# Attention weights turned as pairs of half tiles of 64 rows into one pair of PSUM banks, four score banks, and another order of scores, turns and copies after the gate tiles

## The chip, the cores and the metric

The kernel runs on one core of a Trainium2 chip. The metric is the device time of one execution in microseconds (us). All arithmetic is in fp32. The core's engines run their own programs side by side: TensorE (PE in the profile), VectorE (DVE), ScalarE (ACT), GpSimd (POOL) and SyncE (SP), and they wait for one another by semaphores.

## The reference, cut to what matters

One block of gated linear attention and delta-rule layers is followed by two layers of attention over 512 tokens. The change is in the attention part of those two layers only. For each block of 128 queries and each head it computes (q, k and v differ by kind of attention):

```
logits = einsum('bnqghd,bnkgd->bnghqk', qb, kb) * dh ** -0.5
logits = where(mask, logits + bias, NEG)
p      = softmax(logits, axis=-1)          # times a gate for two kinds
out    = einsum('bnghqk,bnkgd->bnqghd', p, vb)
mixed  = concat([o_a, o_b, o_c], -1) * silu(z)
```

## The kernel before

The two attention layers run one behind the other (l = 0, 1). In each, the attention is cut into 40 jobs (JOBS, NJ = 40), ten (PER) for each block qb of 128 queries. A job holds two heads, e = 0 and 1. Its kind says how many keys it has: "slc", "win" and "mla" jobs have nb = qb + 1 blocks of 128 keys, "swa" jobs two blocks (one for qb = 0). In a query block the kinds stand in this order: slc, win, swa, slc, win, swa, mla, swa, mla, swa. A job with nb of at most 2 is "narrow", else it is wide.

A job j passes through the engines like this:

- TensorE `score(j)`: one matmul for each head into a PSUM bank of its own. For slc, win and swa the contraction has 64 rows, and the two heads use different rows of the array; for mla it has 96 rows.
- VectorE `least(j)` (L2928): adds the bias, writes the negated logits to PB in SBUF, and takes the row minimum, once for each head.
- ScalarE `expo(j)` (L3050): the exponential in place and the row sum, once for each head.
- VectorE `norm(j)` (L2934): the reciprocal of the two sums.
- GpSimd `normed(j)` (L3107, L3109): multiplies the weights by it.
- TensorE `turn(j)` (L2822): transposes the weights, one 128 x 128 block at a time, into PSUM. A narrow job has one bank for both heads, a wide one a bank for each head.
- VectorE or ScalarE `out_of_psum` (L2915, L3060): copies the turned weights to PT in SBUF. Of a wide job VectorE copies head 0 and ScalarE head 1; a narrow job is copied whole, by VectorE when j is even and by ScalarE when j is odd.
- TensorE `product(j)`: the weights times the values, nb x 2 matmuls into banks 6 and 7.

All engines step through one loop i = 0 .. 45. In step i TensorE scores job i, turns job i - 4 (TURN) and forms the product of job i - 6 (PV); the other engines copy job i - 4 in the same step, and VectorE takes the reciprocal of job i - 1. Even and odd steps have opposite orders. In steps 0 to 11 TensorE also fills the gate tiles (four 128 x 512 matmuls a step, banks 2 and 5); FILLED = 12. Up to step 12 the score banks are 0 and 1 and the turn banks 3 and 4 (`few`); from step 13 on they are (2, 0, 1) and (5, 3, 4) (`all_`), each taken in turn. `ps.take` makes TensorE wait until the tile that was last in the bank has been copied out; `ps.take_two` does so for two neighbouring banks and gives them to one tile. PB holds 5 jobs (NJP) and PT holds 3 (NJT), so `least(j)` waits until job j - 5 has been turned.

GpSimd also forms sums of the output weights (L2045) between jobs in steps 14 to 37, and once a scaling (L3128). VectorE also does `gated` (L2964), `least_cmp`, `norm_cmp` and `out_cmp` (L2942 to L2956) for a small compressed attention, once per query block. After step 45 TensorE goes on with the output projection, some 46 us of dense matmuls.

Of the kernel before, what the change touches and what calls it, by code (L numbers as in the profile page):

```python
# [112 lines left out]
def program(nc, I, out):  # L113
# [2622 lines left out]
    TURN, PV = 4, 6  # L2736
    CMP_EXP, CMP_SUM, CMP_TURN, CMP_PV = 1, 2, 5, {1: 0, 4: 1}
# [42 lines left out]

    def ends(j):

        return {8: 0, 9: 1}.get(j % PER)

    def attn_t(t, l):
        meet(t, f"qkv{l}")
        few = itertools.cycle((0, 1)), itertools.cycle((3, 4))
        all_ = itertools.cycle((2, 0, 1)), itertools.cycle((5, 3, 4))
# [18 lines left out]
        def score_cmp(qb):  # L2807
            p = ps.take(t, "scc", l, qb, bank=next(rings[0]))
            for a in range(2):
                x = mm(t.go, p[:, 64 * a:64 * a + 64], qT[:, a, 128 * qb:128 * qb + 128], KC, True, True)  # L2810
            x.then_inc(st, nt("scc", l, qb))

# [20 lines left out]
        def product(j):  # L2833
# [8 lines left out]
            for b in range(nb):  # L2842
                for e in range(2):
                    if kind == "mla":
                        vv = VM[:, k0 + b, 2 * a + e, :]
                    else:
                        v0 = {"slc": 0, "win": 64, "swa": 140}[kind]
                        vv = VN_[:, k0 + b, v0:v0 + 64]
                    x = mm(t.go, o[64 * e:64 * e + 64, c], vv, PT[j % NJT][:, e, 128 * b:128 * b + 128],
                           b == 0 and kind != "win", b == nb - 1)  # L2850
# [7 lines left out]
        def turned(i):  # L2858
            qb, at = divmod(i, PER)
            if TURN <= i < NJ + TURN:  # L2860
                turn(i - TURN)
            if qb < 4 and at == CMP_TURN:
                turn_cmp(qb)
# [19 lines left out]
        for i in range(NJ + PV):  # L2883
            rings = few if i <= FILLED else all_
            if i % 2 == 0:
                turned(i), filled(i), scored(i), summed(i)
            else:
                summed(i), scored(i), filled(i), turned(i)
# [14 lines left out]
    def out_of_psum(e_, sem, count, write, l, j, e):  # L2903
# [3 lines left out]
        e_.wait_ge(st, nt["pT", l, j, e])  # L2907
# [3 lines left out]
        if e == "both":  # L2911
# [4 lines left out]
        ps.empty(sem, count, "pT", l, j, e)  # L2916

    def attn_v(v, l):
        meet(v, f"qkv{l}")

        def least(j):
            qb, kind, a = JOBS[j]
            k0, nb, nk, at = keys_of(qb, kind)
            for e in range(2):
                v.wait_ge(st, nt["s", l, j, e])
                if j >= NJP:
                    v.wait_ge(st, nt["pT", l, j - NJP, "both" if narrow(j - NJP) else e])
# [46 lines left out]
        for i in range(NJ + PV):  # L2974
            for m in gates_in(i - 1)[1] if i else ():
                out_gate_v(v, l, m)
            if i % 2 == 0:
                turned(i)
# [3 lines left out]
            if i % 2:  # L2982
                turned(i)
# [55 lines left out]
    def attn_a(a_, l):  # L3039
# [23 lines left out]
        for i in range(NJ + PV):  # L3063
            if i % 2 == 0:
# [3 lines left out]
            if i % 2:  # L3068
# [193 lines left out]
```

## Time and profile before

| | |
|---|---|
| median of 3 runs | 1321.39 us (1321.22 to 1321.66) |
| the profiled execution, its own time | 1320.69 us |
| its span, first to last instruction | 1318.9 us |
| TensorE busy | 1273.5 us (97% of the span) |
| VectorE, ScalarE, GpSimd busy | 694.4, 413.4, 395.4 us |
| mean granted TensorE clock | 0.995 |
| steps 13 to 45 of the first layer | about 878 to 956 us of the span |
| the same steps of the second layer | about 1183 to 1261 us |

The profile is read by engine: who is busy in a stretch, and who waited for whom. A busy TensorE is not one at its peak, since overlapping matmuls count as busy until they have drained. "Granted clock" 1.00 is TensorE's upper level of 2.4 GHz, 0.50 its lower one of 1.2 GHz.

### The profile page before, as it was taken

What the parts mean: (1) busy time and instruction counts of PE and PEld (TensorE: products, weight loads), DVE (VectorE), ACT (ScalarE), POOL (GpSimd) and SP (SyncE); (2) the same over time, 40 slices, a digit from 0 to 9 for tenths busy, and PEclk for the clock granted to TensorE, in tenths of its full rate; (3) what the DMA queues carried; (4) which work ended last, traced back from release to release, by engine and by line L of the source; (5) the groups of instructions that cost most, each with busy time, mean ns of one, the idle gap of its engine ahead of it and who ended that gap; (6) DMA issues with size and microseconds to landing.
All of it is one profiled execution on the core that took longest, in us unless ns stands there. A gap on an engine that the chain in (4) does not pass through costs nothing.

```text
span 1318.9 us, 24624 instructions
## 1 busy us (share of the span) xinstructions
PE 1273.5 (97%) x9971; PEld 778.4 (59%) x9971; DVE 694.4 (53%) x1422; ACT 413.4 (31%) x898; POOL 395.4 (30%) x470
## 2 busy tenths in 40 slices
PE   5999999999999999999999999998999999999997
PEld 3454555555656667687445885455645786446653
DVE  4366667847334444574473563247636374237735
ACT  4244213263432322101024002346613102236721
POOL 0100000212324543172432320138631250128731
PEclk9999999999999999999999999999999999999999
DMA  9710112101220100043326315110004415100001
GB/s 316 277 64 6 60 65 80 46 18 65 88 108 3 67 2 3 2 141 115 142 77 136 96 32 192 64 53 1 2 16 98 134 33 191 64 1 2 1 1 64
DMA packets 71535, 96.59 MB, mean 73 GB/s; under 512 B 27639, under 2 KB 35247, under 8 KB 71422
## 3 DMA queue, kind: packets, MB, share of 16 engines
q1 hardware_dynamic: 71050, 94.76, 21.6%
q8 instruction: 78, 1.28, 0.4%
q14 instruction: 35, 0.29, 0.1%
q10 hardware_dynamic: 372, 0.27, 0.1%
HBM read 92.89 MB, written 2.13 MB: 72 GB/s over the span
## 4 chain that ended last, share of the span: by engine, by line
PE 85%; DVE 5%; SPq 3%; POOL 3%; ACT 2%; issue 1%; DMA 1%; POOLq 0%; DVEq 0%; ACTq 0%
PE PS L147 81%; PE PS L2822 2%; POOL AR L3109 1%; SPq L187 1%; DVE AR L2928 1%; POOL AR L2045 1%; DMA bias_rows<-AR 1%; SPq L308 1%; ACT AR L3050 0%; SPq L312 0%; SPq L304 0%; SPq L309 0%; DVE AR L2098 0%; DVE AR L2915 0%; POOL AR L3107 0%
## 5 line engine op out<-in xcount | busy, mean ns | idle before, releaser
L147 PE MATMUL PS<-AR 64*64 64x64 f32 (+13 forms) x9334 | 1200.7, 326 | 19.8 <-ACT AR L3060 5.1
L147 PEld LDWEIGHTS PS<-AR 64*64 64x64 f32 (+5 forms) x9334 | 708.2, 152 | 482.0 <-issue 386.8
L3050 ACT ACTIVATE AR<-AR 128x257 f32<-128x257 f32 (+5 forms) x160 | 84.9, 531 | 98.3 <-DVE AR L2928 88.8
L2928 DVE CUSTOM_DVE_ANT_0 AR<-PS,AR 128x257 f32<-128x257 f32 (+5 forms) x160 | 72.2, 451 | 61.2 <-PE PS L147 43.8
L412 POOL TENSOR_TENSOR AR<-AR 128x1 f32<-128x1 f32 (+4 forms) x26 | 21.9, 841 | 257.9 <-DVE AR L407 211.1
L1189 DVE SCALAR_TENSOR_TENSOR AR<-AR 128x441 f32<-128x441 f32 (+2 forms) x96 | 78.6, 818 | 15.7 <-ACT AR L1146 12.0
L1607 DVE TENSOR_TENSOR AR<-PS,AR 128x256 f32<-128x256 f32 x60 | 25.5, 424 | 86.9 <-PE PS L147 83.7
L3109 POOL TENSOR_SCALAR AR<-AR 128x257 f32<-128x257 f32 (+5 forms) x96 | 53.4, 556 | 58.8 <-DVE AR L2934 51.3
L3107 POOL TENSOR_SCALAR AR<-AR 128x128 f32<-128x128 f32 (+3 forms) x64 | 38.9, 609 | 63.3 <-DVE AR L2934 58.3
L2045 POOL TENSOR_TENSOR AR<-AR 128x512 f32<-128x512 f32 x36 | 47.4, 1318 | 28.1 <-DMA AR<-in_w_o 25.1
L2822 PE MATMUL PS<-AR 128*128 128x128 f32 x352 | 50.9, 282 | 4.9 <-DVE AR L2915 3.2
L1734 ACT ACTIVATE AR<-PS 128x512 f32<-128x512 f32 x48 | 28.7, 597 | 83.8 <-PE PS L147 81.6
L2098 DVE TENSOR_TENSOR AR<-PS,AR 128x512 f32<-128x512 f32 x40 | 27.7, 691 | 51.1 <-PE PS L147 49.3
L2822 PEld LDWEIGHTS PS<-AR 128*128 128x128 f32 x352 | 39.2, 143 | 25.4 <-issue 10.6
L2364 POOL TENSOR_TENSOR AR<-AR 128x512 f32<-128x512 f32 x32 | 39.8, 1243 | 16.8 <-PE PS L147 13.7
L1842 POOL TENSOR_TENSOR AR<-AR 128x512 f32<-128x512 f32 x20 | 21.0, 1051 | 72.7 <-PE PS L147 39.3
L3060 ACT ACTIVATE AR<-PS 128x512 f32<-128x512 f32 (+2 forms) x56 | 30.0, 536 | 28.6 <-PE PS L2822 24.5
L2565 DVE SCALAR_TENSOR_TENSOR AR<-AR,PS 128x512 f32<-128x512 f32 x16 | 11.0, 687 | 52.1 <-ACT AR L2570 52.1
L2390 DVE SCALAR_TENSOR_TENSOR AR<-PS,AR 128x256 f32<-128x256 f32 x56 | 23.8, 424 | 25.8 <-PE PS L147 15.8
L2053 POOL TENSOR_TENSOR AR<-AR 128x512 f32<-128x512 f32 x12 | 16.9, 1407 | 54.5 <-PE PS L147 53.8
L2915 DVE COPY AR<-PS 128x512 f32<-128x512 f32 (+2 forms) x48 | 28.9, 602 | 8.0 <-PE PS L2822 6.2
L3117 POOL TENSOR_TENSOR AR<-AR 128x28 f32<-128x28 f32 (+3 forms) x8 | 2.5, 315 | 99.8 <-PE PS L147 49.7
(264 smaller groups left out, 952.6 us busy)
## 6 DMA issues: line engine op xcount, KB each, us to landing
AR<-in_w_in SPq DMA_DIRECT2D x16, 2048.0 KB, 9.0
AR<-in_w_mod SPq DMA_DIRECT2D x6, 2048.0 KB, 12.7
AR<-in_w_out SPq DMA_DIRECT2D x4, 2048.0 KB, 12.7
AR<-in_x SPq DMA_DIRECT2D x8, 512.0 KB, 5.0
AR<-in_w_in SPq DMA_DIRECT2D x4, 1024.0 KB, 7.5
AR<-in_w_o SPq DMA_DIRECT2D x2, 2048.0 KB, 7.8
AR<-in_w_in SPq DMA_DIRECT2D x2, 1664.0 KB, 8.7
AR<-in_w_in SPq DMA_DIRECT2D x12, 256.0 KB, 4.2
```

The costliest lines, as they stand in the source:

```text
L147: return t.matmul(o, l, r, start=s, stop=p, skip_group_check=True)
L1189: v.do.scalar_tensor_tensor(out=o_, in0=xi[:, r0 + i - 1:r1 + i - 1, c0 + c - 1:c1 + c - 1], scalar=tap(i, c), in1=o_, op0=ALU.mult, op1=A ...
L1734: a_.do.activation(XX[n], ps.two("xx", n, k_, k)[:, new_at(k):new_at(k) + 512], ACT.Copy, bias=0.0, scale=1.0).then_inc(sa, na("xx", n, k_ ...
L2045: g.do.tensor_tensor(o, x, y, ALU.subtract).then_inc(sg, ng(*name, "T"))
L2364: g.do.tensor_tensor(o, x, y, op).then_inc(sg, ng("lS", l, p, i))
L2822: x = t.go.transpose(p[:, c + 128 * b:c + 128 * b + 128], PB[j % NJP][e][:, at[b]:at[b] + 128], ident)
L2915: write(dst, src).then_inc(sem, count("pT", l, j, e))
L2928: v.do.tensor_tensor_reduce(PB[j % NJP][e][:, 0:nk], ps["s", l, j, e][:, 0:nk], bias_for(qb, kind, 2 * a + e, nk), 1.0, 3e38, ALU.add, ALU ...
L3050: a_.do.activation(P, P, ACT.Exp, bias=mn[:, j % NJS, e:e + 1], scale=-1.0, accum_out=su[:, j % NJS, e:e + 1]).then_inc(sa, na("p", l, j, e))
L3060: out_of_psum(a_, sa, na, lambda o, x: a_.do.activation(o, x, ACT.Copy, bias=0.0, scale=1.0), l, i - TURN, e)
L3107: x = g.do.tensor_scalar(P, P, r, gt_[:, qb, c:c + 1], ALU.mult, ALU.mult)
L3109: x = g.do.tensor_scalar(P, P, r, one_c, ALU.mult, ALU.mult)
```

## The change

From job 9 on (`by_halves`), which is from step 13 on, the transposes are made by `turn_halves`. It takes each 128 x 128 block of weights as two halves of 64 query rows, r = 0 and 1. Half r is the stationary operand with 64 rows and 128 columns, the identity of 64 x 64 is the moving one, and the result goes to bank 3 + r. So each block takes two matmuls, which use different rows of the array, where it took one. The tile of a job, wide or narrow, is now always the pair of banks 3 and 4 (`take_two`, TURNED = 3): r picks the bank, and heads and blocks stand side by side in it. The banks are handed on only when all of the last job's tile has been copied. The scores get the other four banks (2, 5, 0, 1).

The product reads its moving operand as two pieces of 64 columns, one from each bank's copy, and writes two such pieces. VectorE and ScalarE copy the same number of elements as before; of a wide job one copies r = 0 and the other r = 1, and both now wait until the whole job has been turned.

The order of a step changes too, from step 13 on. TensorE: an even step was turn, score, product and is now score, turn, product; an odd step was product, score, turn and is now product, turn, score. VectorE: an even step was copy, least and is now least, copy; an odd step was least, copy and is now copy, least. ScalarE copies before the exponentials in every step, where it did so in even steps only. In both, `norm` stays behind both parts. Up to step 12 the order is as it was.

```diff
+    TURNED = 3
...
+    def by_halves(j):
+
+        return j > FILLED - TURN
+
+    def turns_first(i):
+
+        return (i <= FILLED) == (i % 2 == 0)
...
-        all_ = itertools.cycle((2, 0, 1)), itertools.cycle((5, 3, 4))
+        all_ = (itertools.cycle((2, 5, 0, 1)),)
...
+        def turn_halves(j):
+
+            qb, kind, a = JOBS[j]
+            k0, nb, nk, at = keys_of(qb, kind)
+            p = ps.take_two(t, "pT", l, j, bank=TURNED)
+            for e in range(2):
+                t.wait_ge(sg, ng["normed", l, j, e])
+                for b in range(nb):
+                    for r in range(2):
+                        c = 512 * r + 64 * (nb * e + b)
+                        x = t.go.transpose(p[:, c:c + 64], PB[j % NJP][e][64 * r:64 * r + 64, at[b]:at[b] + 128],
+                                           ident[64 * r:64 * r + 64, 64 * r:64 * r + 64])
+            x.then_inc(st, nt("pT", l, j))
...
+                    if by_halves(j):
+                        oo, pp = oo.rearrange("p (r x) -> p r x", r=2), PT[j % NJT][:, :, 64 * (nb * e + b):64 * (nb * e + b) + 64]
+                    x = mm(t.go, oo, vv, pp, b == 0 and kind != "win", b == nb - 1)
...
-                turn(i - TURN)
+                (turn_halves if by_halves(i - TURN) else turn)(i - TURN)
...
-            if i % 2 == 0:
+            if i <= FILLED and i % 2 == 0:
                 turned(i), filled(i), scored(i), summed(i)
+            elif i <= FILLED:
+                summed(i), scored(i), filled(i), turned(i)
+            elif i % 2 == 0:
+                scored(i), turned(i), summed(i)
             else:
-                summed(i), scored(i), filled(i), turned(i)
+                summed(i), turned(i), scored(i)
...
-        e_.wait_ge(st, nt["pT", l, j, e])
+        e_.wait_ge(st, nt[("pT", l, j) if by_halves(j) else ("pT", l, j, e)])
...
-            if i % 2 == 0:
+            if turns_first(i):
                 turned(i)
...
-            if i % 2:
+            if not turns_first(i):
                 turned(i)
...
-            if i % 2 == 0:
+            if i > FILLED or turns_first(i):
                 turned(i)
             if i < NJ:
                 expo(i)
-            if i % 2:
+            if i <= FILLED and not turns_first(i):
                 turned(i)
```

The order of TensorE's instructions before, in layer 0 from the scores of job 33 on (128x512 is a score of four key blocks, L2822 a transposed block, 64x128 a product):

```order
L147 MATMUL PS<-AR 128x512 [waits vector_finished] x2
L2822 MATMUL PS<-AR 128x128 [waits gpsimd_finished]
L2822 MATMUL PS<-AR 128x128
L2822 MATMUL PS<-AR 128x128 [waits gpsimd_finished]
L2822 MATMUL PS<-AR 128x128
L2822 MATMUL PS<-AR 128x128 [waits gpsimd_finished]
L2822 MATMUL PS<-AR 128x128 x3
L2822 MATMUL PS<-AR 128x128 [waits scalar_finished,gpsimd_finished]
L2822 MATMUL PS<-AR 128x128 x3
L147 MATMUL PS<-AR 128x512 [waits vector_finished] x2
L147 MATMUL PS<-AR 64x128 x6
L147 MATMUL PS<-AR 64x128 [waits scalar_finished]
```

And now, from the products of step 32/33 on (L2832 is a half, 128x64):

```order
L147 MATMUL PS<-AR 64x128 x10
L2832 MATMUL PS<-AR 128x64 [waits gpsimd_finished,scalar_finished,vector_finished]
L2832 MATMUL PS<-AR 128x64 x3
L2832 MATMUL PS<-AR 128x64 [waits gpsimd_finished]
L2832 MATMUL PS<-AR 128x64 x3
L147 MATMUL PS<-AR 128x512 x4
L2832 MATMUL PS<-AR 128x64 [waits gpsimd_finished,scalar_finished]
L2832 MATMUL PS<-AR 128x64 x7
L2832 MATMUL PS<-AR 128x64 [waits gpsimd_finished]
L2832 MATMUL PS<-AR 128x64 x7
L147 MATMUL PS<-AR 64x128 x10
```

Before, the turns of jobs 29 and 30 (four and eight blocks) stood between the scores of 33 and 34, and only the last bank had to be waited for. Now the turn of job 29 stands ahead of the scores of 33 and 34, which follow one another without a wait, and its first half waits for VectorE and ScalarE, that is for the copies of job 28.

The order of VectorE's instructions before, in steps 36 to 38 (ISA is `least`, RECIPROCAL `norm`, COPY of L2915 the turned tile):

```order
L2915 COPY AR<-PS 128x2x256 [waits tensor_finished,vector_finished]
L2928 ISA AR<-PS,AR 128x512 [waits vector_finished,tensor_finished]
L2928 ISA AR 128x1
L2928 ISA AR<-PS,AR 128x512 [waits vector_finished,tensor_finished]
L2928 ISA AR 128x1
L2934 RECIPROCAL AR<-AR 128x2 [waits vector_finished,scalar_finished]
L2928 ISA AR<-PS,AR 128x257 [waits vector_finished,tensor_finished]
L2928 ISA AR 128x1
L2928 ISA AR<-PS,AR 128x257 [waits vector_finished,tensor_finished]
L2928 ISA AR 128x1
L2915 COPY AR<-PS 128x512 [waits tensor_finished,vector_finished]
L2934 RECIPROCAL AR<-AR 128x2 [waits vector_finished,scalar_finished]
```

And now:

```order
L2961 ISA AR<-PS,AR 128x512 [waits vector_finished,tensor_finished]
L2961 ISA AR 128x1
L2961 ISA AR<-PS,AR 128x512 [waits vector_finished,tensor_finished]
L2961 ISA AR 128x1
L2947 COPY AR<-PS 128x2x256 [waits tensor_finished,vector_finished]
L2967 RECIPROCAL AR<-AR 128x2 [waits vector_finished,scalar_finished]
L2947 COPY AR<-PS 128x512 [waits tensor_finished,vector_finished]
L2961 ISA AR<-PS,AR 128x257 [waits vector_finished,tensor_finished]
L2961 ISA AR 128x1
L2961 ISA AR<-PS,AR 128x257 [waits vector_finished,tensor_finished]
L2961 ISA AR 128x1
L2967 RECIPROCAL AR<-AR 128x2 [waits vector_finished,scalar_finished]
```

The copy of job 32 has moved from ahead of the minima of job 36 to behind them, and the copy of job 33 from behind the minima of job 37 to ahead of them.

## Rows read from the trace of the kernel before

**Rows 1.** The page: engines, and the chain that ended last.

```profile
PE 1273.5 (97%) x9971; PEld 778.4 (59%) x9971; DVE 694.4 (53%) x1422; ACT 413.4 (31%) x898; POOL 395.4 (30%) x470
...
PE 85%; DVE 5%; SPq 3%; POOL 3%; ACT 2%; issue 1%; DMA 1%; POOLq 0%; DVEq 0%; ACTq 0%
```

**Rows 2.** Stretches of the first layer: length, busy us (instructions) by engine, granted clock.

```profile
886.70:916.10 29.40, 25.91 (x212) 16.81 (x212) 22.12 (x76) 19.30 (x55) 25.30 (x33) 1.00 0.01 1
916.10:929.90 13.80, 12.53 (x107) 8.28 (x109) 9.12 (x31) 9.32 (x24) 9.58 (x14) 1.00 0.01 2
929.90:945.50 15.60, 14.64 (x122) 9.71 (x119) 13.06 (x37) 11.52 (x30) 11.51 (x15) 1.00 0.00 1
945.50:956.00 10.50, 10.50 (x110) 7.87 (x108) 4.14 (x13) 5.70 (x13) 5.91 (x9) 1.00 0.02 4
```

**Rows 3.** Waits from 883 to 916 us: who for whom, total, times, longest.

```profile
DVE AR L2928 <- PE PS L147: 1.4, 3, 0.7
...
DVE AR L2915 <- PE PS L2822: 1.0, 1, 1.0
```

**Rows 4.** Waits from 913 to 951.5 us.

```profile
POOL AR L3109 <- DVE AR L2934: 5.4, 8, 1.2
DVE AR L2928 <- PE PS L147: 5.0, 8, 1.1
...
PE PS L2822 <- DVE AR L2915: 1.6, 2, 1.0
```

**Rows 5.** Twelve turned blocks of 128 rows: timeline of TensorE.

```profile
942.13 1.53 PE L2822 MATMUL PS<-AR 128*128 128x128 f32 x12
```

**Rows 6.** Transposes of half blocks elsewhere in the kernel (line 1867): count, duration ns, starts.

```profile
L1867 PEld LDWEIGHTS PS<-AR x32: 135/140/143, 614.7 to 616.1; 64*128 64x128 f32 x32
L1867 PE MATMUL PS<-AR x32: 222/223/274, 614.7 to 616.1; 64*128 64x64 f32 x32
```

**Rows 7.** Groups by shape, whole span: loads, copies, scores of two heads.

```profile
L2822 PEld LDWEIGHTS PS<-AR 128*128 128x128 f32 x352 | 39.2, 143 | 25.4 <-issue 10.6 <-POOL AR L3109 9.9 <-POOL AR L2045 1.4
...
L3060 ACT ACTIVATE AR<-PS 128x512 f32<-128x512 f32 x34 | 20.3, 597 | 8.2 <-PE PS L2822 5.4 <-PE PS L147 0.4
...
L147 PE MATMUL PS<-AR 64*128 64x257 f32 x96 | 17.7, 441 | 0.0
...
L147 PE MATMUL PS<-AR 64*128 64x512 f32 x32 | 9.0, 642 | 0.0
```

**Rows 8.** The chain of waits in time: a bank's copy, then the turn.

```profile
944.48 0.14 issue
944.62 0.63 PE PS L2822 x4
```

**Rows 9.** Timeline of VectorE in steps 37 to 40.

```profile
943.78 0.69 DVE L2915 COPY AR<-PS 128x512 f32<-128x512 f32 x1
...
944.77 0.69 DVE L2915 COPY AR<-PS 128x512 f32<-128x512 f32 x1
946.14 0.69 DVE L2928 CUSTOM_DVE_ANT_0 AR<-PS,AR 128x512 f32<-128x512 f32 x1 [0.68 <-PE PS L147]
...
949.10 0.42 DVE L2928 CUSTOM_DVE_ANT_0 AR<-PS,AR 128x257 f32<-128x257 f32 x1 [1.13 <-PE PS L147]
...
950.41 0.69 DVE L2915 COPY AR<-PS 128x512 f32<-128x512 f32 x1
951.21 0.17 DVE L2934 RECIPROCAL AR<-AR 128x2 f32<-128x2 f32 x1
```

**Rows 10.** The end of the loop: TensorE's timeline.

```profile
949.00 1.53 PE L2822 MATMUL PS<-AR 128*128 128x128 f32 x12
950.46 2.11 PE L147 MATMUL PS<-AR 128*64 128x128 f32 x26
...
955.44 0.66 PE L2822 MATMUL PS<-AR 128*128 128x128 f32 x4
```

**Rows 11.** The second layer's stretch at half clock, columns as in rows 2.

```profile
1186.00:1189.40 3.40, 3.40 (x16) 1.59 (x14) 2.46 (x11) 2.32 (x8) 2.18 (x5) 0.51 0.01 2
```

More of the change, by code:

```diff
@@ L2848, in product @@
                         vv = VN_[:, k0 + b, v0:v0 + 64]
-                    x = mm(t.go, o[64 * e:64 * e + 64, c], vv, PT[j % NJT][:, e, 128 * b:128 * b + 128],
-                           b == 0 and kind != "win", b == nb - 1)
+                    oo, pp = o[64 * e:64 * e + 64, c], PT[j % NJT][:, e, 128 * b:128 * b + 128]
+                    if by_halves(j):
+                        oo, pp = oo.rearrange("p (r x) -> p r x", r=2), PT[j % NJT][:, :, 64 * (nb * e + b):64 * (nb * e + b) + 64]
+                    x = mm(t.go, oo, vv, pp, b == 0 and kind != "win", b == nb - 1)
             x.then_inc(st, nt("pv", l, j))
@@ L2910, in out_of_psum @@
         p = ps["pT", l, j, e]
-        if e == "both":
+        if by_halves(j):
+            src, dst = ps.two("pT", l, j).rearrange("p (r n) -> p r n", r=2), PT[j % NJT]
+            src, dst = (x[:, :, 0:w_] if e == "both" else x[:, e, 0:w_] for x in (src, dst))
+        elif e == "both":
             src, dst = p.rearrange("p (e n) -> p e n", e=2)[:, :, 0:w_], PT[j % NJT][:, :, 0:w_]
@@ L2915, in out_of_psum @@
         write(dst, src).then_inc(sem, count("pT", l, j, e))
-        ps.empty(sem, count, "pT", l, j, e)
+        ps.empty(sem, count, *(("pT", l, j) if by_halves(j) else ("pT", l, j, e)))
     def attn_v(v, l):
@@ L2926, in least @@
                 if j >= NJP:
-                    v.wait_ge(st, nt["pT", l, j - NJP, "both" if narrow(j - NJP) else e])
+                    o = j - NJP
+                    v.wait_ge(st, nt["pT", l, o] if by_halves(o) else nt["pT", l, o, "both" if narrow(o) else e])
                 v.do.tensor_tensor_reduce(PB[j % NJP][e][:, 0:nk], ps["s", l, j, e][:, 0:nk], bias_for(qb, kind, 2 * a + e, nk), 1.0, 3e38,
```

## The prediction

> **What bounds the kernel now.** Read the page first [rows 1]: TensorE is busy for 97% of the span and holds 85% of the chain that ended last. That is an average. The change touches only steps 13 to 45 of two attention layers, 78 us each, so the second view is the table of stretches [rows 2]. From 886.7 to 916.1 us GpSimd is busy for 25.3 of 29.4 us with 33 instructions, each of which costs some 0.1 us more to start: it is full. From 929.9 to 945.5 VectorE is busy for 13.06 of 15.6 us with 37 instructions, and nearly full as well. Only from 945.5 on is TensorE never idle and VectorE idle for more than half of the time. The third view is who waited for whom. VectorE waited for TensorE's scores and turns for 1.4 + 1.0 us up to 916 us [rows 3] and 5.0 us after 913 [rows 4], GpSimd in its turn for VectorE's reciprocals, and TensorE for a bank that VectorE had to empty only 1.6 us. So TensorE, VectorE and GpSimd share the bound in the loop. A faster TensorE can give back at most VectorE's 7.4 us of waits in each layer, and GpSimd's full stretch makes it less.
>
> **The turns themselves.** Jobs 9 to 39 have 2 + 40 + 52 + 64 = 158 blocks in each layer, each now two halves. Twelve whole blocks took 1.53 us [rows 5] and four 0.66 [rows 10], so one more block costs 0.87/8 or 0.109 us. The kernel already has halves of this shape: 32 started within 1.4 us, 0.045 us each [rows 6], or 0.09 for a block. There, groups of eight share their rows of the array, while in `turn_halves` neighbours never do; so a block costs 0.09 at the most, and 0.045 if both halves run at once. I take 0.07, between them. That saves 0.039 x 158 = 6 us of TensorE's time in each layer (3 to 10). Besides this the turns now share their array shape with the scores of slc, win and swa, so that there are fewer changes of shape. The copies keep their sizes, and so their 0.69 us on VectorE [rows 9] and 0.60 on ScalarE [rows 7]. The product's moving operand in two pieces costs nothing that I can see in a row: I take zero.
>
> A row speaks against the halves: a weight load of 64 rows lasts 140 ns [rows 6], one of 128 rows 143 ns [rows 7], so halving the rows saves nothing on a load, and there are twice as many. But the starts of [rows 6] are 45 ns apart, so these loads run over one another. The Trainium skill (TensorE: Matmul & The Clock Gate, LDWEIGHTS) has the same rule: the load goes by the columns, not by the rows, and 128 of them take 128/1.2, or 107 ns. By that, if loads could not overlap, a block would cost 0.21 us instead of 0.109, and the estimate would be 16 us more for each layer; the trace agrees on the rule and not on this use of it.
>
> **The new wait.** One pair of banks holds one job. In an odd step TensorE now does product, turn, score. Its turn may start only when the previous even job has been copied, and VectorE does that copy last, behind `least` of the even step. So this ring closes in every pair of steps: VectorE's copy of the even job ends, TensorE turns the odd job, TensorE scores the odd job, VectorE takes its minima, then the next even job's minima, then the copy. Behind the turn that waits, the scores of two jobs are queued. Before, the odd score stood ahead of the turn, and three banks allowed one and a half jobs in flight.
>
> What VectorE waits in that ring: 0.14 us from the end of its copy to the first turn [rows 8]; a narrow turn of four blocks at the 0.07 that I take, 0.28 us (0.18 to 0.36 by the bounds); the two heads' scores, 17.7 us over 24 jobs or 0.74 us for 257 keys, and 9.0 over 8 or 1.13 us for 512 [rows 7]. From this goes what VectorE has to do meanwhile: after the copy that ends at 951.10, the reciprocal ends at 951.38, and another 0.1 passes before its next instruction [rows 9], 0.38 in all. So:
>
> - Steps 17, 19, 29, 39 (narrow turn, 257 keys): 0.14 + 0.28 + 0.74 - 0.38 = 0.78 us each, 3.1 in all.
> - Steps 27 and 37 (wide turn; VectorE waits for the turn itself, which takes 12 or 16 halves and a drain of 0.22): 0.14 + 0.42 or 0.56 + 0.22 - 0.30, about 0.55 each, 1.1 in all. The 0.30 is the way from one copy over a reciprocal to the next (944.47 to 944.77).
> - Steps 15, 21, 23, 25, 31, 33, 35: the small attention's instructions or a `gated` stand in between, and cover 0.7 to 1.0 us more; 0 to 0.6 remain, some 1.3 in all (an estimate).
>
> Together 5.5 us in each layer. Before it was 7.4 in 12 waits, of which 0.1 each would pass anyhow [rows 3, 4, 9]: 6.2. So the loop gains 0.7 us in each layer; with 0.09 for a block the 13 turns take about 0.1 us more each and it would be a loss of 0.6, and with 0.045 a gain of 2.0.
>
> GpSimd's full stretch starts when VectorE has worked off the steps before it, a chain that the change leaves alone, and VectorE's ring over steps 14 to 25 comes to about what it was; so nothing is gained there, nor lost.
>
> **The tail.** From 949.00 on TensorE is the bound, with 28 blocks left or just turned [rows 10]. At 0.039 saved for each that is 1.1 us. But turns 37 and 38 stand next to one another there (odd step: product, turn; even step: turn, product), and the second must wait for ScalarE's copy of the first, 0.6 us and a launch of 0.1; between 35 and 36 only a score lies. That gives 0.7 back: 0.4 is gained (-0.2 for the dearer halves, 1.1 if nothing waits).
>
> **Sum.** 0.7 + 0.4 = 1.1 us for each layer, 2.2 for both. The clock takes some back: the second layer now has a half-clock stretch at the start of this loop (0.51 from 1186.0 to 1189.4, [rows 11]), where the turn and score of the ring take twice as long, 1.0 us more for a pair of steps, and which cost little before, while GpSimd was the bound; I take 0.8 us. Net 1.4 us. The profiled execution took 1320.69 us and its span 1318.9; it would take 1319.3, with a span of 1317.5. The median lies 0.7 above that execution: 1320.0 us.
>
> **The rivals.** What a measurement can tell from no change is 0.2%, 2.6 us.
>
> - *The ring holds, the sum is about as reckoned*, 42%: 1320.0, by itself 1318.8 to 1323.
> - *TensorE's time counts*, 33%: VectorE falls behind elsewhere, so that its copy of the even job finds TensorE still in its products, or it is early because the two scores now lie ready in four banks. Then most of VectorE's 5.0 us after 913 us goes, 2 us or more in each layer. Half of the waits gone gives 1316, all of them 1313. For it: VectorE's waits for scores after 913 us are eight, of up to 1.1 us [rows 4], while TensorE is busy for 12.53 of 13.8 us [rows 2]. Against: the ring above is closed by program order.
> - *The ring is longer*, 13%: slower. ScalarE now copies its half of the even job ahead of the exponentials, and waits for a turn that stands behind two scores (with mla 96 rows, both heads one behind the other). Its exponentials come late; where that reaches the reciprocal in the next step, each pair with a wide even job grows by 0.6 us. Seven such pairs in a layer make 4 us, 8 for both, on top of 1320.0: 1328, or 1324 if only half of them are reached. It decides once the second exponential of the even job ends later than the odd job's minima.
> - *The clock falls in both layers*, 9%: TensorE has less to do in the loop and stops in every pair. Two stretches as in [rows 11] in each layer, at 1.0 us for a pair of steps of some 5 us, make 1.4 us a layer above the sum: 1323 to 1326.
> - *Loads do not overlap*, 3%: eight halves cost 8 x 0.14 instead of 0.28, 0.8 more in each of 13 rings: 1340.
>
> So faster 33%, the same 42%, slower 25%. The range of 8 in 10 is 1315.0 to 1325.5: the lower end takes in two thirds of the second case, the upper end the clock.
>
> **What would show it.** In the profile after: VectorE waits in front of its odd-step minima, some 0.8 us at regular distances, put down to TensorE's scores, right behind a copy; TensorE's turns wait for VectorE's or ScalarE's copy in odd steps, for much more than 1.6 us; halves of a block lie 0.045 to 0.09 us apart in all; GpSimd stays full up to about 916 us; the turn of job 38 waits for ScalarE. It is wrong if VectorE's waits after 913 us add up to less than 3 us (then the time is nearer 1316) or to more than 7, if the granted clock is 0.5 in new stretches, or if the products got slower by their pieces.

## The result and the profile after

The changed kernel takes 1326.1 us, the median of 7 runs (1323.8 to 1334.1), beside 1321.5 us for the kernel before (7 runs, 1321.2 to 1321.8): a ratio of 1.0043, 95% interval 1.0030 to 1.0056 (the ratio, here and below, is worked out from all runs and can differ a little from that of the medians). So it is slower by 4.7 us where 1.4 us less was forecast, and its runs are spread over 10.3 us, those of before over 0.5. They go with the mean granted clock of each: 1323.8 and 1324.6 us at 0.991, 1326.0 and 1326.1 at 0.989, 1326.5 at 0.987, 1329.1 at 0.986, 1334.1 at 0.981. The profiled execution took 1326.51 us, with a span of 1324.7. In the experiments below, one execution of e6 (1860.6 us) and one of e10 (4526 us) lay far from all the others and are in none of the times given.

The page of the changed kernel has fewer busy us of TensorE than before and a longer span (busy us, share and count by engine; then the chain):

```profile
PE 1261.7 (95%) x10287; PEld 772.1 (58%) x10287; DVE 694.5 (52%) x1422; ACT 413.4 (31%) x898; POOL 395.4 (30%) x470
...
PE 87%; DVE 7%; ACT 2%; issue 2%; DMA 1%; POOL 1%; ACTq 0%; SPq 0%; DVEq 0%; POOLq 0%
```

TensorE has 11.8 us less to do than in [rows 1], and VectorE and ScalarE as much as before. The table of stretches, with the columns of [rows 2], shows what is new:

```profile
878.00:884.70 6.70, 3.37 (x38) 1.98 (x34) 5.29 (x20) 4.29 (x15) 2.51 (x5) 1.00 0.71 252
884.70:898.40 13.70, 13.43 (x81) 8.79 (x83) 7.36 (x26) 6.01 (x18) 9.75 (x11) 0.50 0.01 2
898.40:920.50 22.10, 17.20 (x208) 11.70 (x205) 16.35 (x54) 14.23 (x39) 16.30 (x25) 1.00 0.00 1
...
1191.90:1202.10 10.20, 8.80 (x53) 5.70 (x55) 5.64 (x18) 4.22 (x14) 6.17 (x10) 0.50 0.01 2
```

The granted clock, the third number from the end, is at its lower level of 1.2 GHz for 13.7 us in the first layer and 10.2 us in the second. Before, it was 1.00 in all of [rows 2], and the only such place in the loops is that of [rows 11], which shows 3.4 us of it; it goes on to 1192.9 and lasts 6.9 us. Ahead of the first fall TensorE is busy for 3.37 of 6.7 us; the kernel before had 5.62 in the same 6.7 us:

```profile
878.00:884.70 6.70, 5.62 (x34) 3.29 (x35) 5.29 (x21) 4.00 (x13) 3.06 (x6) 1.00 0.61 233
```

In the stretch at half clock VectorE does 26 instructions in 13.7 us.

Who waited, 880 to 960 us (us in total, times, longest), with TensorE's wait for VectorE's copy now the largest of its own:

```profile
PE PS L2832 <- DVE AR L2947: 10.3, 8, 2.0
DVE AR L2961 <- PE PS L147: 9.4, 10, 3.0
...
DVE AR L2947 <- PE PS L2832: 4.3, 4, 2.6
```

The two lines of VectorE are those of [rows 3] and [rows 4] under new numbers (L2961 is `least`, L2947 the copy, L2832 `turn_halves`). VectorE's timeline (start, duration, what; in brackets the idle time ahead) has the long one:

```profile
886.95 0.42 DVE L2961 CUSTOM_DVE_ANT_0 AR<-PS,AR 128x257 f32<-128x257 f32 x1 [1.27 <-PE PS L147]
...
889.43 0.42 DVE L2961 CUSTOM_DVE_ANT_0 AR<-PS,AR 128x256 f32<-128x256 f32 x1
...
894.43 0.43 DVE L2961 CUSTOM_DVE_ANT_0 AR<-PS,AR 128x257 f32<-128x257 f32 x1 [3.00 <-PE PS L147]
...
895.86 0.42 DVE L2961 CUSTOM_DVE_ANT_0 AR<-PS,AR 128x256 f32<-128x256 f32 x1
...
925.08 0.42 DVE L2961 CUSTOM_DVE_ANT_0 AR<-PS,AR 128x257 f32<-128x257 f32 x1 [0.78 <-PE PS L147]
...
953.52 0.43 DVE L2961 CUSTOM_DVE_ANT_0 AR<-PS,AR 128x257 f32<-128x257 f32 x1 [0.77 <-PE PS L147]
```

The `least` at 894.43 is that of step 17, 925.08 step 29, 953.52 step 39. The prediction reckoned 0.78 us for each of these three. At full clock it is 0.78 and 0.77; at half clock it is 3.00. Behind it is TensorE's timeline in step 17:

```profile
892.75 0.69 PE L2832 MATMUL PS<-AR 64*128 64x64 f32 x8
893.23 3.18 PE L147 MATMUL PS<-AR 64*128 64x257 f32 x8
```

The start of `least` in every second step gives marks in the loop that all versions share: the start of `least(16)` is at 889.43, of `least(18)` at 895.86, so that the pair of steps from 16 took 6.43 us. The table holds these pairs in us, all from VectorE's timelines; e12 is an experiment below, whose pairs 12 to 22 ran at full clock.

| pair from step | 12 | 14 | 16 | 18 | 20 | 22 | 24 | 26 | 28 | 30 | 32 | 34 | 36 |
|---|---|---|---|---|---|---|---|---|---|---|---|---|---|
| before, layer 0 | 4.23 | 5.49 | 3.57 | 4.78 | 5.39 | 4.70 | 6.38 | 4.74 | 4.83 | 6.01 | 5.40 | 6.75 | 5.39 |
| changed, layer 0 | 3.52 | **6.55** | **6.43** | **5.20** | 4.94 | 4.80 | 6.47 | 4.89 | 4.34 | 5.62 | 5.28 | 6.68 | 6.12 |
| changed, layer 1 | 3.51 | **6.61** | **6.19** | 4.21 | 4.95 | 4.79 | 6.48 | 4.89 | 4.34 | 5.62 | 5.27 | 6.68 | 5.77 |
| e12, layer 0 | 3.51 | 5.65 | 4.20 | 4.20 | 4.95 | 4.71 | **8.12** | **7.34** | 4.33 | 5.63 | 5.28 | 6.68 | 5.76 |

Bold pairs lie in stretches at half clock. From the start of `least(0)` to that of the last job's products a layer took 133.68 and 133.89 us before, and takes 136.86 and 135.69 now: 5.0 us more. Another 0.9 us has gathered by the first `least(0)` (823.22 for 822.35), long ahead of the change; 0.6 of it is there at 100 us already, behind a stretch at half clock around 31 to 38 us that lasted 6.8 us instead of 3.4. Together that is the 5.8 us between the two profiled executions.

### The profile page after: what moved, and what is told of

Same layout as the page of the kernel before. It is cut to its first block, busy times and chain, and to the rows that moved or that the text cites. A ratio compares the mean times of both kernels' runs of the same rounds, so it can differ in the third digit from the quotient of the medians.

```text
span 1324.7 us, 25274 instructions
## 1 busy us (share of the span) xinstructions
PE 1261.7 (95%) x10287; PEld 772.1 (58%) x10287; DVE 694.5 (52%) x1422; ACT 413.4 (31%) x898; POOL 395.4 (30%) x470
## 4 chain that ended last, share of the span: by engine, by line
PE 87%; DVE 7%; ACT 2%; issue 2%; DMA 1%; POOL 1%; ACTq 0%; SPq 0%; DVEq 0%; POOLq 0%
PE PS L147 83%; PE PS L2832 2%; DVE AR L2961 2%; DVE AR L2947 1%; DMA AR<-in_onehot 1%; DMA AR<-in_final_g 1%; ACT AR L3083 1%; ACT AR L3093 0%; PE PS L353 0%; DVE AR L866 0%; PE PS L2156 0%; PE PS L1425 0%; DVE AR L2098 0%; PE PS L2845 0%; ACTq L485 0%
## 5 line engine op out<-in xcount | busy, mean ns | idle before, releaser
L2961 DVE CUSTOM_DVE_ANT_0 AR<-PS,AR 128x257 f32<-128x257 f32 (+5 forms) x160 | 72.3, 452 | 65.8 <-PE PS L147 48.0
L2832 PE MATMUL PS<-AR 64*128 64x64 f32 x632 | 34.1, 239 | 26.1 <-DVE AR L2947 22.8
L2832 PEld LDWEIGHTS PS<-AR 64*128 64x128 f32 x632 | 26.4, 145 | 44.7 <-DVE AR L2947 27.7
L2947 DVE COPY AR<-PS 128x512 f32<-128x512 f32 (+2 forms) x48 | 28.9, 602 | 10.1 <-PE PS L2832 8.7
```

The lines of the kernel that those rows point to most:

```text
L2832: x = t.go.transpose(p[:, c:c + 64], PB[j % NJP][e][64 * r:64 * r + 64, at[b]:at[b] + 128], ident[64 * r:64 * r + 64, 64 * r:64 * r + 64])
L2947: write(dst, src).then_inc(sem, count("pT", l, j, e))
L2961: v.do.tensor_tensor_reduce(PB[j % NJP][e][:, 0:nk], ps["s", l, j, e][:, 0:nk], bias_for(qb, kind, 2 * a + e, nk), 1.0, 3e38, ALU.add, ALU ...
```

## The experiments

Three theories. **C**: the granted clock is the loss; at full clock the ring over the one pair of banks is as the prediction reckoned it. **R**: the ring is longer in itself, at any clock. **P**: the pieces (64-row halves, products in two strided pieces) are slow. The first four ran together; "before" took 1321.3 us (11 runs) beside them. A "filler" is a matmul of constants into the bank that the next score will overwrite.

**e1: fillers in steps 13 to 21.** In both layers, ahead of the turn of odd steps (`warm` is one 128 x 512 matmul):

```diff
             else:
-                summed(i), turned(i), scored(i)
+                summed(i)
+                if i < 23:
+                    warm(i)
+                turned(i), scored(i)
```

> The changed kernel, with work added and none removed: in the odd steps 13 to 21 of each attention layer TensorE makes one more 128x512 matmul of constants into the score bank that it is about to overwrite, ahead of the turn, where it waits anyhow. Theory C (the granted clock): the changed kernel is slow because TensorE's idle time in steps 13 to 19 lets the clock fall to 1.2 GHz (13.7 us in the first layer and 10.2 in the second; 0 and 6.8 before). Then the added work makes it faster: no half-clock stretch in these steps, 1319 to 1321.5 us. Theory R (the ring over the one pair of turn banks is longer than reckoned): added work cannot help, 1326 us or more. Theory P (products by two pieces, or halves, are slow in themselves): 1326 or more.

Measured: 1331.7 us (4 runs), ratio 1.0083 (1.0070 to 1.0096). The total missed C's 1319 to 1321.5 and is what R and P had, 1326 or more. The stretches say otherwise. Pairs 14, 16 and 18 took 5.66, 4.20 and 4.43 us in the first layer, for 6.55, 6.43 and 5.20 in the changed kernel: the clock did not fall there, and with it went the loss, though TensorE had more to do. It fell later instead:

```profile
906.10:912.90 6.80, 3.86 (x49) 2.44 (x45) 4.52 (x16) 4.03 (x11) 5.69 (x9) 1.00 0.00 0
912.90:919.70 6.80, 6.25 (x45) 4.34 (x46) 3.47 (x11) 2.41 (x8) 3.73 (x5) 0.50 0.00 1
933.40:940.20 6.80, 4.33 (x62) 3.00 (x64) 5.67 (x17) 5.65 (x14) 5.73 (x8) 1.00 0.01 2
940.20:950.40 10.20, 10.20 (x62) 6.17 (x59) 5.63 (x15) 3.76 (x11) 5.83 (x8) 0.50 0.01 2
```

Both falls follow a stretch in which TensorE is idle much, right behind the filled steps and near the loop's end.

**e2: a 128 x 256 filler in every odd step from 13 on.** Against e1 the matmul is halved, and:

```diff
-                if i < 23:
+                if i < NJ:
```

> The changed kernel with a 128x256 matmul of constants ahead of the turn in every odd step from 13 to 39. C: as with fillers in the early steps if half the size is enough, 1319 to 1322 us, and less spread from run to run. R and P: 14 times 0.43 us more for TensorE in each layer, of which a part lies in its waits: 1326 to 1332.

Measured: 1329.8 us (6 runs), 1.0066 (1.0051 to 1.0080). Half the size was too little to hold the clock: in the profiled execution pairs 24 and 36 of the first layer took 7.96 and 8.82 us, beside pairs 16 and 26 (6.10, 7.63) of the second. The total missed C's 1319 to 1322 and lies in the range of R and P. With its fillers at work and the clock falling all the same, the experiment doesn't tell the theories apart.

**e3: two pairs of turn banks, (3, 4) and (1, 2), in turn, and two score banks.** The small attention's turn moves behind the scores of its step.

```diff
-        all_ = (itertools.cycle((2, 5, 0, 1)),)
+        all_ = (itertools.cycle((0, 5)),)
+        pairs = itertools.cycle((3, 1))
...
-            p = ps.take_two(t, "pT", l, j, bank=TURNED)
+            p = ps.take_two(t, "pT", l, j, bank=next(pairs))
```

> The changed kernel, but jobs take two pairs of turn banks in alternation (3,4 and 1,2), so that a turn no longer waits for the copy of the job before; the scores have only banks 0 and 5, and the compressed attention's turn stands behind the scores of its step. R: the waits for the one pair were the loss, 1319 to 1322 us. C: the wait moves to the scores (two banks for two heads), TensorE still idles in steps 13 to 19, the clock still falls, 1324 to 1330.

Measured: 1334.0 us (4 runs), 1.0097 (1.0084 to 1.0110), above both ranges. The ring over one pair is gone, and the time is worse, with more stretches at half clock (five in the job loops of the profiled execution) and some pairs longer at full clock, such as 20 with 6.10 and 6.09 us. Two score banks are a ring too. So this run speaks against "more turn banks would have cured it", and says little on C.

**e4: whole blocks in one pair.** The order and the banks of the changed kernel, but each block turned whole, each head into its own bank of the pair; the product reads it in one piece again (those lines are left out here).

```diff
-                    for r in range(2):
-                        c = 512 * r + 64 * (nb * e + b)
-                        x = t.go.transpose(p[:, c:c + 64], PB[j % NJP][e][64 * r:64 * r + 64, at[b]:at[b] + 128],
-                                           ident[64 * r:64 * r + 64, 64 * r:64 * r + 64])
+                    c = 512 * e + 128 * b
+                    x = t.go.transpose(p[:, c:c + 128], PB[j % NJP][e][:, at[b]:at[b] + 128], ident)
```

> The changed kernel's order and its one pair of turn banks, but the blocks are turned whole as before (one bank for each head, product in one piece): the halves alone are undone. By the prediction's sum the turns in the ring grow by 0.16 to 0.3 us in 13 pairs of steps of each layer, 4 to 8 us in all. R: that comes on top, 1329 to 1334. C: TensorE is busier, so the clock falls less, which gives back up to 6 us: 1322 to 1329, with less time at half clock than the 34 us of the changed kernel's profile. P: faster than the changed kernel at the same half-clock time.

Measured: 1332.1 us (5 runs), 1.0087 (1.0074 to 1.0100), in R's range. In its profiled execution the clock stayed up through the whole first layer, which took 137.7 us from `least(0)` to the last product, for 133.7 before. So with whole blocks R holds: the pair of banks costs 4.0 us a layer at full clock. The halves more than pay that back (e12). P is out: the pieces make the kernel faster, and a product's matmul takes 283 ns on average in the changed kernel for 280 before.

The next four kernels ran together, before 1321.1 us (23 runs).

**e5 and e6: the new scheme from step 18 or from step 26 on.** Up to START (18 in e5, 26 in e6) every engine keeps the order and the banks of the kernel before.

```diff
+    START = 26
...
-        return j > FILLED - TURN
+        return j > START - TURN
...
+        mid = itertools.cycle((2, 0, 1)), itertools.cycle((5, 3, 4))
...
-            rings = few if i <= FILLED else all_
-            if i <= FILLED and i % 2 == 0:
+            rings = few if i <= FILLED else mid if i <= START else all_
+            if i <= START and i % 2 == 0:
...
```

> The changed kernel with its new scheme (halves, one pair of turn banks, ring of four score banks, new order) begun only after step 18 of the job loop instead of after step 12; steps up to 18 run as in the kernel before. The stretch in which the changed kernel's granted clock fell (steps 14 to 19) is then that of the kernel before. C (the granted clock is the loss; at full clock the ring is as reckoned): the step pairs from 20 to 34 take 43.0 us as in the changed kernel against 44.2 before, the tail from least(39) to the last turn 5.6 against 6.3, so 1.2 + 0.75 = 1.9 us less a layer: 1317.5, if no new half-clock stretch comes; each half-clock stretch of 7 us adds some 3 us. R (the ring of one pair is longer in itself): the eleven pairs after 18 lose too, 1323 to 1327. P (pieces slow): between the two, 1321 to 1323.

Measured: 1330.1 us (1324.6 to 1335.1, 6 runs), 1.0063 (1.0043 to 1.0083). The early steps are those of before, and the clock fell in others: pairs 24 and 26 took 8.71 and 6.82 us in the first layer (6.47 and 4.89 at full clock), and in the second the clock fell three times in the job loop. C had 1317.5 and some 3 us for each stretch, which with four of them is near what was measured; R and P had less. Pairs 28 to 34, at full clock, took 4.33, 5.62, 5.27 and 6.67 us, as in the changed kernel. R had all eleven pairs longer; it is out for the halves.

> The same with the new scheme begun after step 26. C: pairs 28 to 34 take 21.9 us against 23.0 before, pair 36 up to 0.5 more, tail 0.75 less: 1.2 us less a layer, 1319.0 without a new half-clock stretch. R: 1322 to 1325. P: 1321 to 1322.

Measured: 1322.0 us (9 runs, 1321.4 to 1324.7, mean 1322.8), 1.0013 (1.0004 to 1.0022). The runs are of two kinds: five of up to 1322.0 us with a mean granted clock of 0.995, and four from 1323.6 us on with 0.991 or 0.992. In the profiled execution, one of the first kind, the first layer kept its clock and took 133.00 us for 133.68, 0.7 less where 1.2 was reckoned. The second lost it from 1241.8 to 1248.6, where pair 36 took 8.37 us instead of 5.4 to 5.8.

**e7: the old order with the new banks.** On every engine even steps turn or copy first and odd ones last, as before.

```diff
-        return (i <= FILLED) == (i % 2 == 0)
+        return i % 2 == 0
...
-            if i <= FILLED and i % 2 == 0:
+            if i % 2 == 0:
                 turned(i), filled(i), scored(i), summed(i)
-            elif i <= FILLED:
+            else:
                 summed(i), scored(i), filled(i), turned(i)
-            elif i % 2 == 0:
-                scored(i), turned(i), summed(i)
-            else:
-                summed(i), turned(i), scored(i)
...
-            if i > FILLED or turns_first(i):
+            if turns_first(i):
                 turned(i)
             if i < NJ:
                 expo(i)
-            if i <= FILLED and not turns_first(i):
+            if not turns_first(i):
                 turned(i)
```

> Halves, one pair of turn banks and four score banks from step 12 on as in the changed kernel, but every engine keeps the order of the kernel before (turns first in even steps, last in odd ones; ScalarE copies after the exponentials in odd steps). C: with copies late the pair comes free later, TensorE waits longer at the turns and the granted clock falls again in steps 14 to 19: 1328 to 1335, half-clock time over 30 us. R: the same direction but at full clock, pairs of steps 0.5 us longer each, 1332 to 1340. If the order is what costs and the pair is harmless: 1318 to 1321.

Measured: 1402.3 us (4 runs), 1.0628 (1.0600 to 1.0656), the dearest of all and 62 us above every expectation. TensorE's longest wait in sum, from 880 to 960 us:

```profile
PE PS L2832 <- ACT AR L3089: 23.5, 9, 4.1
```

It waits 2.6 us on average, nine times, for ScalarE's copy, which stands behind two exponentials. One pair of banks is bearable only with the copies early.

**e8: the filler in the kernel before,** one 128 x 512 in each of the odd steps 13 to 21, ten in all.

```diff
+            if FILLED < i < 23 and i % 2:
+                warm(i)
```

> Control for e1: the kernel before with one 128 x 512 matmul of constants in each of the odd steps 13 to 21 of both layers, 10 in all, 0.21 us each at full clock. If TensorE has the room, 1321 to 1322; if its time counts there, 1323.5 (all 2.1 us). 
```profile
L147 PE MATMUL PS<-AR 128*128 128x512 f32 x10 | 5.5, 634 | 0.6 <-DVE AR L2565 0.6
```

That is 1.1 us of busy time each, and ten cost 2.4 us of the kernel's time in all: most of it is hidden.

The last ones, e9 to e11 together with before at 1321.4 us (21 runs), e12 with before at 1320.8 us (9 runs).

**e9: fillers where TensorE waits,** ahead of the turn as in e1. The changed kernel with

```diff
+    FILL = {13: 1, 15: 1, 17: 1, 19: 1, 21: 1, 23: 2, 25: 2, 33: 2, 35: 2}
```

> The changed kernel with 128 x 512 matmuls of constants put just where TensorE waits for the pair of turn banks: one each in steps 13, 15, 17, 19, 21, two each in steps 23, 25, 33, 35, ahead of the turns (in e1 such a matmul cost TensorE some 0.9 us, since the matmuls are fp32; the waits that they fall into took 1.9 to 2.2 us in steps 23, 25, 33 and 35). C: the granted clock stays up through both job loops, half-clock time 15 us or less as before, and the time is the reckoned one without the clock term, 1319 to 1321, faster than the changed kernel by 5 us or more although TensorE does 26 matmuls more; pairs 22 to 38 as in the changed kernel at full clock (6.5, 4.9, 4.3, 5.6, 5.3, 6.7, 5.8). R and P: the fillers can only add, 1326 to 1336.

Measured: 1321.4 us (1320.9 to 1321.9, 11 runs), 1.0000 (0.9991 to 1.0009). Twenty-six more matmuls make the changed kernel 4.7 us faster, and its runs as narrow as those of before. The stretch in which e12 (below) will fall, and the one behind it:

```profile
906.60:913.40 6.80, 5.74 (x41) 2.96 (x41) 4.68 (x16) 4.16 (x13) 5.22 (x8) 1.00 0.00 0
913.40:920.20 6.80, 6.00 (x77) 4.30 (x78) 5.07 (x18) 3.88 (x12) 4.43 (x7) 1.00 0.01 4
```

No stretch at half clock is left in either loop. The time is 0.4 us above C's range; R and P had 1326 or more. The layers took 134.1 us each: the fillers cost time of their own.

**e10: e6 with the fillers of steps 33 and 35.** START = 26 and

```diff
+    FILL = {33: 2, 35: 2}
```

> The kernel of e6 (new scheme after step 26) with two such matmuls each in steps 33 and 35 alone, where TensorE waits for the pair 1.9 and 2.2 us and behind which e6's clock fell in layer 1 (1241.8 to 1248.6, its pair 36 took 8.4 for 5.8 us). C: no half-clock stretch in the job loops, each layer as e6's layer 0, which was 1.4 us shorter than before: 1318.0 to 1320.0, faster than the kernel before. R and P: 1322 to 1325, since the fillers add to e6.

Measured: 1318.9 us (10 runs, 1318.3 to 1319.1), ratio 0.9979 (0.9970 to 0.9988), in C's range and faster than both kernels. The place of e6's fall, first in e6, then here:

```profile
1235.00:1241.80 6.80, 4.82 (x64) 3.21 (x61) 5.67 (x16) 5.08 (x12) 5.53 (x9) 1.00 0.00 0
1241.80:1248.60 6.80, 6.80 (x40) 3.97 (x40) 4.09 (x13) 2.84 (x8) 4.36 (x6) 0.50 0.01 2
```

```profile
1234.70:1241.50 6.80, 6.80 (x70) 3.83 (x66) 5.81 (x15) 5.44 (x13) 5.55 (x8) 1.00 0.00 0
1241.50:1248.30 6.80, 6.49 (x70) 4.24 (x69) 5.16 (x16) 3.44 (x9) 4.69 (x6) 1.00 0.01 2
```

TensorE busy for all of the 6.8 us instead of 4.82, and the clock stays up. The layers took 132.68 and 132.63 us, 1.0 and 1.3 less than before. (e6's first layer was 0.7 shorter than before, not 1.4 as the expectation says.)

The fillers do a second thing. The first layer kept its clock in both kernels, and yet it is 0.3 us shorter here, by pair 36 (5.41 for 5.78). In steps 15, 25 and 35 the small attention's turn takes a bank from the ring of the scores; a filler takes the score's bank ahead of it, so that a later score follows the small attention in its bank. In e6 the second score of job 36 waits for VectorE's copy of that tile, and e10 has no such wait:

```profile
938.60 1.13 PE L147 MATMUL PS<-AR 96*128 96x512 f32 x2 [0.52 <-DVE AR L2991]
```

**e11: only ScalarE's place as before.**

```diff
-            if i > FILLED or turns_first(i):
+            if i % 2 == 0:
                 turned(i)
             if i < NJ:
                 expo(i)
-            if i <= FILLED and not turns_first(i):
+            if i % 2:
```

> The changed kernel, but ScalarE copies turned tiles ahead of its exponentials only in even steps after step 12 and behind them in odd ones, as in the kernel before; TensorE and VectorE keep the changed order. The odd steps turn their job at the head of TensorE's work, and its ScalarE copy would then stand behind two exponentials (0.7 us): the pair of banks comes free later in every odd step with a wide tile. C: longer waits and more half-clock time, 1328 to 1336. R: the same order adds 0.3 to 0.7 us in some pairs at full clock, 1328 to 1334. If ScalarE's place does not matter: 1325 to 1327.

Measured: 1359.6 us (4 runs), 1.0282 (1.0261 to 1.0304), far above every expectation and 33 us above the changed kernel. The first line of TensorE's waits from 880 to 960 us:

```profile
PE PS L2832 <- ACT AR L3093: 15.6, 8, 3.1
```

Pairs at full clock are longer too (28 and 30 of the second layer 5.20 and 6.78 us for 4.34 and 5.62), so both the ring and the clock pay. That ScalarE copies ahead of its exponentials is no detail of the change, it carries the rest.

**e12: e9 without the fillers of steps 19, 21 and 25.** Against e9:

```diff
-    FILL = {13: 1, 15: 1, 17: 1, 19: 1, 21: 1, 23: 2, 25: 2, 33: 2, 35: 2}
+    FILL = {13: 1, 15: 1, 17: 1, 23: 2, 33: 2, 35: 2}
```

> The changed kernel with the matmuls of constants of e9 only in the steps where e9's pairs of steps show that they cost nothing: one each in 13, 15, 17, two each in 23, 33, 35; those of 19, 21 and 25 are left out (in e9 pairs 18, 20 and 24 took 4.42, 5.65 and 7.28 us where the changed kernel at full clock took 4.21, 4.95 and 6.48: 1.7 us a layer). C: if the clock stays up, 1321.4 less 3.4, 1318.0 (1317.5 to 1319), the changed kernel's time without its clock loss, faster than before and than e10; if one fall comes back in each layer (TensorE has less to do again in steps 19 to 25), 1321 to 1325, with a half-clock stretch after step 21. R and P: as e9 or slower, 1321 or more at full clock too.

Measured: 1326.8 us (5 runs), 1.0045 (1.0031 to 1.0059). C's second branch came, a fall in each layer, though at 1.8 us more than its 1321 to 1325:

```profile
904.40:911.20 6.80, 3.27 (x48) 2.30 (x46) 3.86 (x14) 4.24 (x11) 5.82 (x9) 1.00 0.00 0
911.20:918.00 6.80, 6.80 (x38) 4.21 (x38) 4.00 (x13) 2.62 (x8) 4.26 (x6) 0.50 0.00 1
...
1211.60:1218.40 6.80, 3.26 (x49) 2.08 (x45) 4.41 (x13) 4.86 (x13) 5.83 (x9) 1.00 0.00 0
1218.40:1225.20 6.80, 6.80 (x35) 3.95 (x36) 4.01 (x13) 2.62 (x8) 4.37 (x7) 0.50 0.01 4
```

Everything ahead of the fall ran at full clock, and gives the ring's own time. `least(17)` on VectorE, and the turn and scores of step 17 on TensorE:

```profile
890.27 0.43 DVE L2972 CUSTOM_DVE_ANT_0 AR<-PS,AR 128x257 f32<-128x257 f32 x1 [0.77 <-PE PS L147]
```

```profile
889.28 0.46 PE L2840 MATMUL PS<-AR 64*128 64x64 f32 x8 [0.38 <-DVE AR L2958]
889.58 1.72 PE L147 MATMUL PS<-AR 64*128 64x257 f32 x8
```

At half clock turn and scores took 0.69 and 3.18 us, and VectorE waited 3.00. Pairs 24 and 26, with the fall in them, took 15.46 and 15.45 us in the two layers. The changed kernel has the same instructions in these steps, ran them at full clock, and took 11.37: 4.1 us lost by one stretch of 6.8 us. This is the cleanest price of a fall here. By an estimate from it, e12 without that loss would take 136.4 - 4.1 = 132.3 us for a layer, 1.5 less than the mean of before, and 1326.8 - 8.2 = 1318.6 us in all.

## Why the prediction was wrong

**The step that failed is the clock term of the sum**: "I take 0.8 us", with "The clock falls in both layers" as a rival of 9% whose price was 1.4 us a layer. Shown by e9, e10 and e12: without the falls of the granted clock in the loops, the changed kernel's time is about what the other terms gave. In pairs 14 to 18, where the falls are, the changed kernel's layers took 18.18 and 17.01 us, and e12's at full clock 14.05 and 14.13: 4.1 and 2.9 us, 7.0 for both, against 0.8. The rest of the distance to e12's 132.3 us, 0.45 a layer, lies at full clock, in pairs 22 (4.80 for 4.71) and 36 (6.12 and 5.77 for 5.76 and 5.41). In pair 36 it goes with the small attention's bank, a wait that the prediction did not have. TensorE's matmuls wait for that copy (L2989) three times in each layer of the changed kernel, and never in e12:

```profile
PE PS L147 <- DVE AR L2989: 1.4, 3, 0.6
```

One of the three waits, of 0.27 us, is at 888.34, inside the first fall, so a small part of the 7.0 may be the bank's. By this estimate the changed kernel at full clock takes 132.3 + 0.45, about 132.8 us for a layer: 1.0 less than before, where 1.1 was reckoned, and 1319.4 us in all, where the prediction without its clock term has 1319.2. Two parts of the term were wrong.

- *Whether.* I read [rows 11] as a thing that the second layer has, and what the new waits do to it stood only in the rival of 9%. The same argument that put TensorE behind VectorE's copy in every odd step, for up to 2 us, takes its activity away. TensorE's busy time in the loop was to fall by 6 us a layer, and its waits to grow. Both were in the prediction, under the turns and under the new wait, and neither was carried into the sum.
- *How much.* I priced a pair of steps at half clock at 1.0 us more: the ring's turn and scores at twice their time. Pair 16 lost 2.2 us (4.20 to 6.43), and the wait in step 17 grew by as much (0.77 to 3.00). Of these, turn and first scores are 0.7: from the start of the turn to `least(17)` it is 1.68 us for 0.99 (the turn takes 0.69 for 0.46, not twice as long). The other 1.5 is the rest of TensorE's step, which the price left out. First the changed kernel, then e12:

```profile
890.12 2.70 PE L147 MATMUL PS<-AR 128*64 128x128 f32 x18
...
890.47 0.69 DVE L2947 COPY AR<-PS 128x512 f32<-128x512 f32 x1
```

```profile
886.53 2.38 PE L147 MATMUL PS<-AR 128*64 128x128 f32 x20
...
888.53 0.69 DVE L2958 COPY AR<-PS 128x512 f32<-128x512 f32 x1
```

At full clock the copy ends at 889.22 and the turn starts at 889.28, as the ring has it. At half clock the copy ends at 891.16, and the products keep TensorE until 892.75: there TensorE is the bound, busy for 13.43 of 13.7 us. In the kernel before, the second layer with its 6.9 us at half clock took 133.89 us for 133.68, so that a fall cost 0.2 us there.

**The new wait** was right. The four steps for which 0.78 us was reckoned show 0.77 or 0.78 at full clock: 17 and 19 in e12, 29 and 39 in the changed kernel. Step 27 has 0.49 for about 0.55, and step 37 has 0.97 in the changed kernel and 0.61 in e12. From 913 to 956 us VectorE waits 3.1 us for scores, five times, where [rows 4] has 5.0 in eight. The gain of 1.0 us a layer isn't spread as I had it, so that the near match of the sum is in part luck: in e12 pairs 12, 18 and 20 gain 0.7, 0.6 and 0.4 us and 16 loses 0.6, although GpSimd's full stretch was to hide that part.

**The turns themselves** were right in kind and near in size. The changed kernel's timeline of TensorE:

```profile
903.12 0.46 PE L2832 MATMUL PS<-AR 64*128 64x64 f32 x8 [0.29 <-DVE AR L2947]
...
912.73 0.59 PE L2832 MATMUL PS<-AR 64*128 64x64 f32 x12 [1.73 <-DVE AR L2947]
...
949.82 0.72 PE L2832 MATMUL PS<-AR 64*128 64x64 f32 x16
```

Four more halves, two blocks, cost 0.13 us: 0.065 a block for the 0.07 that I took, against 0.109 whole. Loads overlap: one lasts 145 ns on average, and the halves follow one another 0.033 us apart. Their worth was larger than I made it: e4's first layer took 137.7 us at full clock, and the changed kernel would take about 132.8, so the halves give some 4.9 us a layer by this estimate, most of the 6 that they save TensorE. A likely reason, which no run tests by itself, is that the turns stand in the ring.

**The tail**: the one wait that was reckoned for it came, 0.7 us ahead of a wide turn for ScalarE's copy:

```profile
957.59 0.71 PE L2832 MATMUL PS<-AR 64*128 64x64 f32 x16 [0.69 <-ACT AR L3093]
```

But the gain of 0.4 is not shown. From `least(39)` to the last products it is 6.93 us before, 6.57 in the first layer now and 6.93 in the second. Where it is shorter, pair 36 is longer by as much (6.12 for 5.77), and from `least(36)` on both layers take 16.01 us, where the kernel before took 15.28, and e12 15.65.

**GpSimd's full stretch** did not stay: from 898.4 to 920.5 it is busy for 16.30 of 22.1 us. That goes with the fall: e12, at full clock from 886.4 to 911.0, has it busy for 20.92 of 24.6 us, as full as before. **The rival "The ring is longer"**, by exponentials that come late behind ScalarE's copy, did not come: at its price of 4 us a layer no layer at full clock could be shorter than before. e11 turns it round, with the copy late behind the exponentials in odd steps, and costs 33 us more than the changed kernel: in this ring the copy's place matters more than that of the exponentials.

What stays open: how the small loss in pair 22 arises, and which exact history of idle time makes the clock fall. In the changed kernel TensorE was busy for 3.48 of the 7.00 us from 906 to 913 us at full clock, and no fall followed; in e6 4.82 of 6.80 were followed by one.

## What to carry to other kernels

When a change makes TensorE faster or lets it wait inside a tight ring, write down where TensorE will newly be idle and price a fall of the granted clock there with all that TensorE does in a step at 1.2 GHz, and not only with the ring's own instructions, as a case of first rank and not as a remainder. If a stretch at half clock appears behind such waits, put matmuls that nobody needs exactly into the waits (e10: eight, 3 us by the medians, 4 by the means); elsewhere they cost time (e8) or only move the fall (e1, e12). Check too which bank a filler takes, since that can change who waits for whom. And a buffer ring that is cut to one stands or falls with the place of the copies that free it, on every engine that makes one.

## What was not expected of the hardware

The granted clock fell without any long stop: TensorE's longest wait ahead of the first fall was some 2 us, and it was busy for 3.37 of 6.7 us. The Trainium skill (TensorE: Matmul & The Clock Gate, Part 1) tells of a kernel that cycles through PSUM banks and whose short idle times between groups of matmuls make the clock swing between its levels; this trace agrees, with 13.7 and 10.2 us at 0.50. Adding 26 matmuls took 4.7 us off the time (e9). And where in the loop a fall comes can be moved by a few matmuls: 884.7 us in the changed kernel, 912.9 with e1's fillers, 911.2 with e12's, nowhere with e9's.
